# In the down half of a turn ScalarE rounds the weight pieces of a step before the squared activations of that step

## Chip, cores and metric

The kernel runs on one core of one Trainium2 chip. The metric is the device time of one launch in microseconds, and the time of a kernel is the median of its runs.

## The reference

One layer of a decoder trunk with two parallel branches, for 1024 positions of width 1024, in float32. The branches, their gates and the output projection come first. The change lies in the last part, the feed-forward layer with a squared ReLU:

```python
z = rmsnorm(h, norm_mlp[l])
h = h + jnp.square(jax.nn.relu(z @ w_up[l])) @ w_down[l]     # 1024 -> 4096 -> 1024
return rmsnorm(h, norm_final)
```

## The kernel before

**Numbers in two parts.** TensorE multiplies rounded numbers (fp32r). To keep the precision, every operand x is split into a high part, hi = x rounded, and a low part, lo = x - hi. One product is then three matmuls: hi·hi, hi·lo and lo·hi (lines 799 to 801). The high part of an operand is a Copy activation of ScalarE. The low part is a subtraction on VectorE or on GpSimd, which must wait for the high part.

**Turns and steps.** The first 512 of the 4096 hidden features are done by two plain blocks. The other 3584 are done in 7 turns of 512 features. A turn forms its 2x2 block products by seven products instead of eight (`PRODUCTS`, a Strassen-like scheme), so that sums and differences of weight blocks ("pieces") and of activation quarters are needed. A turn has 28 steps (`PIECES = 28`), and TensorE does 12 matmuls in each. The steps 0 to 13 are the up half (z times pieces of `w_up`, into the PSUM tile `aux`). The steps 14 to 27 are the down half: product m (0 to 6) has two steps, k = 0 and 1. In step 14 + q, with q = 2m + k, TensorE takes the squared activations number q from the slot q % 3 of `h_ring` as stationary operand, and piece 14 + q as moving operand, and adds to `acc` (m even) or `aux` (m odd).

**The five engines.** All of them run the same steps s = 0 to 27 with their instructions in an order written out by hand, and semaphores hold them together. Each engine executes in order, so an instruction that waits holds up everything behind it.

- SyncE loads piece p into its slot of a ring of 7 raw buffers (`p_a`, `p_b`, `p_c`) when TensorE has finished with piece p - 7 (`released`).
- GpSimd (`pieces`) forms the sums of pieces (lines 767, 774, 778; in `sum_at` it is fixed at which step), and the low parts of the pieces 0 to 2 and 18 to 27 (line 756; `lo_at`). Within a step the low parts come first and then the sums. From step 14 on its order is: sum 18 (step 14), sums 19 and 20 (15), low part 18 and sum 21 (16), low parts 19 and 20 and sum 22 (17), low part 21 and sum 23 (18), low parts 22, 23 and so on, low part 27 and sum 29 (24), low part 28 (25), low part 29 and sums 30 and 31 (26). Pieces from 28 on are the pieces 0, 1, ... of the next turn.
- ScalarE (`win_block` in its program) copies and squares quarters in the up half. It rounds the pieces (`cast_pieces(s)`, line 1761: the piece p with `cast_at(p) == s`) and the squared activations (`hidden_hi(q)`, line 1805, in step s = q + 12 for q from 3 on). The cast of piece 18 belongs to step 15, those of 19 and 20 to step 16, then one piece in each step to step 25, and 30 and 31 in step 27.
- VectorE forms the low parts of the pieces 3 to 17 (line 2595), those of the activations (`hidden_lo(q)`, line 2602, in step q + 12), the sums and differences of activation quarters (`hidden_s3`, `hidden_s1`, `hidden_s2`, `hidden_s4`, lines 2609, 2614, 2619, 2625), and it adds finished products from PSUM to the residual `h_res` (`add_pair`, line 2634, 1024 columns in one instruction). Its order around the change is: low parts 1 and 2 of the activations (step 14); `hidden_s3(1)`, `hidden_s1(1)`, `hidden_lo(3)`, `add_pair(0, 0)` (15); `add_pair(0, 1)`, `hidden_s2(1)`, `hidden_lo(4)` (16); `hidden_lo(5)`, `add_pair(1, 0)` (17); and at the end of the turn `hidden_s4(0)`, `hidden_lo(12)` (24) and `hidden_s4(1)`, `hidden_lo(13)` (25).
- TensorE starts step 14 + q when piece 14 + q has its low part (`piece_ready`) and `hidden_lo(q)` is done (`h_ready`).

`hidden_hi(3)` reads the difference that `hidden_s3(1)` writes, and `hidden_hi(5)` what `hidden_s2(1)` writes; `hidden_hi(12)` and `hidden_hi(13)` read what the two `hidden_s4` write. The others only need that TensorE is done with the slot of `h_ring`:

```python
if q >= HRING:
    released(act, UP_PIECES + q - HRING, g)      # TensorE has done step 14 + q - 3
sums = {1: (1, 4), 2: (3, 6), 4: (2, 5), 6: (7, 8)}.get(m)
```

Of the kernel before, what the change touches and what calls it, by code (L numbers as in the profile page):

```python
# [75 lines left out]
def kind(p):  # L76

    r = p % PIECES
    return r % N_PROD if r < UP_PIECES else (r - UP_PIECES) // 2


def chain_of(p):

    r = p % PIECES
    return r // N_PROD if r < UP_PIECES else r % 2
# [6 lines left out]
def cast_at(p):  # L92
    return p - (3 if kind(p) == 2 else 4)
# [6 lines left out]
def summed(p):  # L100
    return SUMS * (p // PIECES) + sum(kind(x) in (1, 2, 3, 4) for x in range(p % PIECES + 1))
# [65 lines left out]
def build(nc, t):  # L167
    with ExitStack() as ctx:
# [298 lines left out]
        def ring(p):  # L467

            s = p % RING
            slot = t_a[:, s] if s < 4 else t_b[:, s - 4] if s < 6 else t_c[:]  # L470
            return slot[:, 0, :], slot[:, 1, :]

        def piece_raw(p):
            s = p % RING
            return (p_a[:, s] if s < 4 else p_b[:, s - 4] if s < 6 else p_c[:])[:, 1, :]

        def released(eng, p, g):

            r, turn = p % PIECES, p // PIECES
            if r < UP_PIECES:  # L480
                eng.wait_ge(prod, g * UP_PIECES + (UP_PIECES * turn + r + 1))
            elif r % 2 == 0:
                eng.wait_ge(half_way, g * N_PROD + (N_PROD * turn + kind(r) + 1))
            else:
                eng.wait_ge(out_ready, g * PIECES + (PIECES * turn + OUT_WIN + 4 * (kind(r) + 1)))

        def quarter(q, k):
            return hid_raw[:, q, k, :]
# [837 lines left out]
        def _(act):  # L1326
# [424 lines left out]
            def cast_pieces(s, g, more=True):  # L1751

                for p in range(s, s + 5):
                    if p >= 0 and (p < PIECES or more) and cast_at(p) == s:
                        if kind(p) in (1, 2, 3, 4):
                            act.wait_ge(t_summed, g * SUMS + summed(p))
                        else:
                            act.wait_ge(ring_in[p % RING], g * 64 + 16 * (p // RING + 1))
                        hi, lo = ring(p)
                        src = t_raw[:, chain_of(p), :] if kind(p) in (1, 2) else piece_raw(p)  # L1760
                        nc.scalar.activation(hi, src, ACT.Copy).then_inc(t_cast, 1)  # L1761
# [11 lines left out]
            def win_block(g, more):  # L1773

                def copy(s, i):
                    q, bank = ((Q11, (0, 3)[s]), (Q22, 1), (Q21, (0, 3)[s]))[i]
                    act.wait_ge(prod, g * 14 + (7 * s + i + 1))
                    nc.scalar.activation(quarter(q, s), aux[:, bank, :], ACT.Copy).then_inc(copied, 1)

                def square(s, i):  # L1780
                    q = (Q21, Q22, Q11, Q12)[i]
                    n = 4 * s + i + 1
                    if i < 3:
                        act.wait_ge(taken, g * 6 + (3 * s + i + 1))
                        nc.scalar.activation(quarter(q, s), quarter(q, s), ACT.Relu).then_inc(relued, 1)
                    else:
                        act.wait_ge(prod, g * 14 + (7 * s + 7))
                        nc.scalar.activation(quarter(q, s), aux[:, (0, 3)[s], :], ACT.Relu).then_inc(u_taken, 1)
                        act.sem_inc(relued, 1)
                        act.wait_ge(u_taken, g * 2 + (s + 1))  # L1790
                    act.wait_ge(relued, g * 8 + n)
                    nc.scalar.activation(quarter(q, s), quarter(q, s), ACT.Square).then_inc(squared, 1)

                def hidden_hi(q):
                    m, k = q // 2, q % 2
                    hi, lo = h_ring[:, q % HRING, 0, :], h_ring[:, q % HRING, 1, :]
                    if q >= HRING:
                        released(act, UP_PIECES + q - HRING, g)
                    sums = {1: (1, 4), 2: (3, 6), 4: (2, 5), 6: (7, 8)}.get(m)
                    if sums is not None:  # L1800
                        act.wait_ge(h_summed, g * 8 + sums[k])
                    else:
                        act.wait_ge(squared, g * 8 + (SQUARED + 4 * k + {0: 3, 3: 2, 5: 4}[m]))
                    src = h_sum[:, q % HRING, 1, :] if m in (1, 6) else quarter({0: Q11, 2: Q11, 3: Q22, 4: Q21, 5: Q12}[m], k)
                    nc.scalar.activation(hi, src, ACT.Copy).then_inc(h_cast, 1)  # L1805

                for s in range(PIECES):
                    if s == 8:
                        hidden_hi(0)
                    if 15 <= s <= 25:  # L1810
                        hidden_hi(s - 12)
                    for b in range(2):
                        if 1 <= s - 7 * b <= 3:
                            copy(b, s - 7 * b - 1)
                        if 4 <= s - 7 * b <= 7:
                            square(b, s - 7 * b - 4)
                    if s == 13:
                        hidden_hi(1)
                        hidden_hi(2)
                    cast_pieces(s, g, more)  # L1820

            with act.Fori(0, N_WIN - 1) as g:
                win_block(g, True)
            win_block(N_WIN - 1, False)

            last_adds = OUT_WIN + 14 * (N_WIN - 1)
# [973 lines left out]
```

## Time and profile before

| what | value |
|---|---|
| time, median of 3 runs | 1497.07 us (1497.02 to 1497.55) |
| profiled execution: time, span | 1496.87 us, 1494.8 us |
| granted TensorE clock, mean | 0.995 |
| TensorE busy | 1465.8 us, 98% |
| VectorE, ScalarE, GpSimd busy | 66%, 35%, 35% |
| the seven turns | from about 933 us to about 1477 us of the span, 77.7 us each |

The span is that of the profiled execution, from its first to its last instruction; its own time is 2.1 us longer. Busy shares are of the whole span. In rows of the timeline the first number is the start in us from the beginning of the span and the second the time that the instruction took. That time contains whatever held the instruction after it had been issued, which matters below.

### The profile page before, as it was taken

What the parts mean: (1) busy time and instruction counts of PE and PEld (TensorE: products, weight loads), DVE (VectorE), ACT (ScalarE), POOL (GpSimd) and SP (SyncE); (2) the same over time, 40 slices, a digit from 0 to 9 for tenths busy, and PEclk for the clock granted to TensorE, in tenths of its full rate; (3) what the DMA queues carried; (4) which work ended last, traced back from release to release, by engine and by line L of the source; (5) the groups of instructions that cost most, each with busy time, mean ns of one, the idle gap of its engine ahead of it and who ended that gap; (6) DMA issues with size and microseconds to landing.
All of it is one profiled execution on the core that took longest, in us unless ns stands there. A gap on an engine that the chain in (4) does not pass through costs nothing.

```text
span 1494.8 us, 20639 instructions
## 1 busy us (share of the span) xinstructions
PE 1465.8 (98%) x7019; PEld 1210.5 (81%) x7019; DVE 981.0 (66%) x1911; ACT 517.9 (35%) x1003; POOL 519.2 (35%) x349
## 2 busy tenths in 40 slices
PE   9999999999999999999999999999999999999995
PEld 8887888888888888888888888878787878787874
DVE  6898564543467527675624788595958586767678
ACT  7422312400122212241101322545444444444455
POOL 4000001245332332004333003273737373646556
PEclk9999999999999999999999999999999999999998
DMA  7225543282111101003542001333333333333333
GB/s 221 99 90 143 144 109 124 72 279 88 57 43 43 43 29 57 29 29 131 179 176 71 1 29 50 120 99 116 103 112 106 104 108 107 108 107 110 107 111 135
DMA packets 150933, 149.02 MB, mean 100 GB/s; under 512 B 19104, under 2 KB 109904, under 8 KB 150864
## 3 DMA queue, kind: packets, MB, share of 16 engines
q1 hardware_dynamic: 118048, 107.00, 23.2%
q10 hardware_dynamic: 32816, 41.12, 8.5%
q8 instruction: 42, 0.69, 0.2%
q14 instruction: 27, 0.22, 0.0%
HBM read 126.58 MB, written 21.50 MB: 99 GB/s over the span
## 4 chain that ended last, share of the span: by engine, by line
PE 84%; DVE 9%; issue 3%; ACT 2%; POOL 1%; ACTq 1%; DMA 0%; DVEq 0%; POOLq 0%
PE acc L799 19%; PE acc L801 19%; PE acc L800 19%; PE aux L800 7%; PE aux L801 7%; PE aux L799 7%; DVE h_ring L2602 1%; DVE h_res L2634 1%; PE aux L1081 1%; PE aux L1074 1%; PE aux L1084 1%; DVE h_sum L2609 1%; PE aux L964 1%; PE aux L958 0%; PE aux L1069 0%
## 5 line engine op out<-in xcount | busy, mean ns | idle before, releaser
L799 PE MATMUL acc<-z_hi,w_hi 128*128 128x512 f32 x448 | 177.2, 396 | 0.6 <-DVE z_lo L1874 0.6
L801 PE MATMUL acc<-z_hi,w_lo 128*128 128x512 f32 x448 | 174.6, 390 | 0.0
L800 PE MATMUL acc<-z_lo,w_hi 128*128 128x512 f32 x448 | 174.5, 390 | 0.0
L799 PE MATMUL acc<-w_hi,z_hi 128*128 128x512 f32 x384 | 164.4, 428 | 0.0
L801 PE MATMUL acc<-w_hi,z_lo 128*128 128x512 f32 x384 | 150.5, 392 | 0.0
L800 PE MATMUL acc<-w_lo,z_hi 128*128 128x512 f32 x384 | 149.6, 390 | 0.0
L663 POOL CAST w_hi<-stage 128x1024 fp32r<-128x1024 f32 x22 | 27.7, 1259 | 344.2 <-PE acc L801 290.0
L650 POOL TENSOR_SCALAR stage<-stage,nm 128x512 f32<-128x512 f32 x48 | 78.3, 1643 | 168.8 <-PE acc L801 86.0
L767 POOL TENSOR_TENSOR t_raw<-t_raw,p_a 128x512 f32<-128x512 f32 x28 | 39.5, 1409 | 262.3 <-DMA p_a<-in_w_up 157.1
L799 PEld LDWEIGHTS acc<-z_hi,w_hi 128*128 128x128 f32 x448 | 84.1, 188 | 19.8 <-issue 1.5
L801 PEld LDWEIGHTS acc<-z_hi,w_lo 128*128 128x128 f32 x448 | 84.1, 188 | 17.9
L800 PEld LDWEIGHTS acc<-z_lo,w_hi 128*128 128x128 f32 x448 | 84.1, 188 | 16.8
L2589 DVE TENSOR_TENSOR hid_raw<-hid_raw,aux 128x512 f32<-128x512 f32 x42 | 28.9, 688 | 91.5 <-PE aux L801 91.5
L801 PEld LDWEIGHTS acc<-w_hi,z_lo 128*128 128x128 f32 x384 | 72.0, 188 | 16.2
L2602 DVE TENSOR_TENSOR h_ring<-hid_raw,h_ring 128x512 fp32r<-128x512 f32 x70 | 82.2, 1195 | 2.2 <-ACT h_ring L1805 2.2
L800 PEld LDWEIGHTS acc<-w_lo,z_hi 128*128 128x128 f32 x384 | 72.4, 189 | 13.5
L799 PEld LDWEIGHTS acc<-w_hi,z_hi 128*128 128x128 f32 x384 | 72.2, 188 | 13.3
L2634 DVE TENSOR_TENSOR h_res<-h_res,acc 128x1024 f32<-128x1024 f32 x54 | 64.3, 1215 | 2.1 <-PE acc L801 1.7
L1805 ACT ACTIVATE h_ring<-hid_raw 128x512 fp32r<-128x512 f32 x70 | 43.7, 624 | 42.2 <-PE aux L801 19.0
L1761 ACT ACTIVATE t_a<-p_a 128x512 fp32r<-128x512 f32 x70 | 43.5, 622 | 36.8 <-POOL p_a L778 36.8
L665 POOL TENSOR_TENSOR w_lo<-stage,w_hi 128x1024 fp32r<-128x1024 f32 x22 | 55.0, 2500 | 1.8
L1459 ACT ACTIVATE gate_t<-acc 128x512 f32<-128x512 f32 x32 | 19.0, 593 | 105.4 <-PE acc L801 94.6
(417 smaller groups left out, 3879.7 us busy)
## 6 DMA issues: line engine op xcount, KB each, us to landing
stage<-in_w_in SPq DMA_DIRECT2D x28, 512.0 KB, 4.4
p_a<-in_w_up SPq DMA_DIRECT2D x56, 256.0 KB, 2.8
p_a<-in_w_down SPq DMA_DIRECT2D x56, 256.0 KB, 2.6
gate_dram<-gate_t ACTq DMA_DIRECT2D x32, 256.0 KB, 2.1
p_b<-in_w_up SPq DMA_DIRECT2D x28, 256.0 KB, 2.7
p_b<-in_w_down SPq DMA_DIRECT2D x28, 256.0 KB, 2.7
x_in<-in_x SPq DMA_DIRECT2D x8, 512.0 KB, 6.1
stage<-in_w_in SPq DMA_DIRECT2D x32, 128.0 KB, 2.3
```

Of the source, the lines that this page charges most:

```text
L650: ins = nc.gpsimd.tensor_scalar(w[:, i, :], w[:, i, :], nm[:, k0 + i:k0 + i + 1], None, ALU.mult)
L663: nc.gpsimd.tensor_copy(dst_hi, stage[:, s, :]).then_inc(hi_pool, 1)
L665: nc.gpsimd.tensor_tensor(dst_lo, stage[:, s, :], dst_hi.bitcast(F32), ALU.subtract)\
L767: ins = nc.gpsimd.tensor_tensor(tmp_raw, tmp_raw, raw_lo, ALU.subtract)
L799: nc.tensor.matmul(out, s_hi, m_hi_, start=first, stop=False, skip_group_check=partial)
L800: nc.tensor.matmul(out, s_hi, m_lo_, start=False, stop=False, skip_group_check=partial)
L801: return nc.tensor.matmul(out, s_lo, m_hi_, start=False, stop=last, skip_group_check=partial)
L1761: nc.scalar.activation(hi, src, ACT.Copy).then_inc(t_cast, 1)
L1805: nc.scalar.activation(hi, src, ACT.Copy).then_inc(h_cast, 1)
L2589: V.tensor_tensor(quarter(q, s), quarter(q, s), aux[:, bank, :], ALU.add).then_inc(taken, 1)
L2602: V.tensor_tensor(lo, src, hi.bitcast(F32), ALU.subtract).then_inc(h_ready, 1)
L2634: V.tensor_tensor(rows, rows, (acc, aux)[m % 2][:, 2 * b:2 * b + 2, :], ALU.add).then_inc(out_free, 1)
```

## The change

In the steps 15 to 27 ScalarE executes `cast_pieces(s)` at the top of the step, ahead of `hidden_hi(s - 12)`. Before, it came last in the step. The steps 0 to 14 stay as they were. No instruction is added or removed, no semaphore count changes, and the other engines' programs are the same.

```diff
                 for s in range(PIECES):
                     if s == 8:
                         hidden_hi(0)
+                    if s >= 15:
+                        cast_pieces(s, g, more)
                     if 15 <= s <= 25:
                         hidden_hi(s - 12)
                     for b in range(2):
...
                     if s == 13:
                         hidden_hi(1)
                         hidden_hi(2)
-                    cast_pieces(s, g, more)
+                    if s < 15:
+                        cast_pieces(s, g, more)
```

## Rows read from the trace of the kernel before

**Rows 1.** The page: busy time of each engine over the span.

```profile
PE 1465.8 (98%) x7019; PEld 1210.5 (81%) x7019; DVE 981.0 (66%) x1911; ACT 517.9 (35%) x1003; POOL 519.2 (35%) x349
```

**Rows 2.** The waits from 900 to 1490 us: who waited for what.

```profile
PE acc L799 <- DVE h_ring L2602: 5.7, 5, 1.1
...
PE acc L799 <- POOL t_b L756: 2.1, 2, 1.1
```

**Rows 3.** The timeline of TensorE, second turn, around step 18.

```profile
1057.42 0.39 PE L799 MATMUL aux<-t_a,h_ring 128*128 128x512 f32 x1
...
1059.91 0.39 PE L801 MATMUL aux<-t_a,h_ring 128*128 128x512 f32 x1
1061.45 0.49 PE L799 MATMUL acc<-t_b,h_ring 128*128 128x512 f32 x1 [1.14 <-DVE h_ring L2602]
...
1064.31 0.39 PE L799 MATMUL acc<-t_b,h_ring 128*128 128x512 f32 x1
```

**Rows 4.** The timeline of the other engines, second turn, steps 14 to 17.

```profile
1048.88 1.30 POOL L774 TENSOR_TENSOR t_raw<-t_raw,p_b 128x512 f32<-128x512 f32 x1 [0.63 <-DVE t_a L2595]
...
1051.05 0.64 ACT L1792 ACTIVATE hid_raw<-hid_raw 128x512 f32<-128x512 f32 x1
...
1051.26 1.68 POOL L774 TENSOR_TENSOR t_raw<-t_raw,p_b 128x512 f32<-128x512 f32 x1 [1.09 <-DVE t_a L2595]
1051.70 1.79 DVE L2602 TENSOR_TENSOR h_ring<-h_sum,h_ring 128x512 fp32r<-128x512 f32 x1
1052.23 3.00 SPq L611 DMA_DIRECT2D p_a<-in_w_down  x2
1052.91 1.73 POOL L778 TENSOR_TENSOR p_c<-p_c,t_raw 128x512 f32<-128x512 f32 x1
1053.42 1.77 DVE L2609 TENSOR_TENSOR h_sum<-hid_raw 128x512 f32<-128x512 f32 x1
1055.22 0.69 DVE L2614 TENSOR_TENSOR hid_raw<-hid_raw 128x512 f32<-128x512 f32 x1
1055.29 0.63 ACT L1805 ACTIVATE h_ring<-h_sum 128x512 fp32r<-128x512 f32 x1 [3.60 <-DVE h_sum L2609]
1055.83 0.62 ACT L1761 ACTIVATE t_b<-t_raw 128x512 fp32r<-128x512 f32 x1
1055.95 0.69 DVE L2602 TENSOR_TENSOR h_ring<-h_sum,h_ring 128x512 fp32r<-128x512 f32 x1
...
1056.52 1.30 POOL L756 TENSOR_TENSOR t_b<-t_raw,t_b 128x512 fp32r<-128x512 f32 x1 [1.88 <-ACT t_b L1761]
1056.57 2.35 DVE L2634 TENSOR_TENSOR h_res<-h_res,acc 128x1024 f32<-128x1024 f32 x2
...
1058.83 0.79 DVE L2619 TENSOR_TENSOR hid_raw<-hid_raw 128x512 f32<-128x512 f32 x1
1059.03 1.74 POOL L756 TENSOR_TENSOR t_b<-t_raw,t_b 128x512 fp32r<-128x512 f32 x1
1059.54 1.77 DVE L2602 TENSOR_TENSOR h_ring<-hid_raw,h_ring 128x512 fp32r<-128x512 f32 x1
```

**Rows 5.** The page: DMA issues of down pieces, KB each, median us to landing.

```profile
p_a<-in_w_down SPq DMA_DIRECT2D x56, 256.0 KB, 2.6
```

**Rows 6.** The timeline, second turn, steps 24 to 27.

```profile
1079.22 1.29 POOL L767 TENSOR_TENSOR t_raw<-t_raw,p_a 128x512 f32<-128x512 f32 x1 [1.23 <-DMA p_a<-in_w_up]
1079.45 1.60 DVE L2625 TENSOR_TENSOR h_sum<-hid_raw 128x512 f32<-128x512 f32 x1
...
1082.38 1.29 POOL L756 TENSOR_TENSOR t_a<-p_a,t_a 128x512 fp32r<-128x512 f32 x1 [1.87 <-ACT t_a L1761]
1082.43 1.79 DVE L2625 TENSOR_TENSOR h_sum<-hid_raw 128x512 f32<-128x512 f32 x1
...
1084.98 0.69 DVE L2602 TENSOR_TENSOR h_ring<-h_sum,h_ring 128x512 fp32r<-128x512 f32 x1 [0.76 <-ACT h_ring L1805]
...
1086.07 0.39 PE L799 MATMUL acc<-t_c,h_ring 128*128 128x512 f32 x1
```

## The prediction, made before the changed kernel was built

> **What bounds the kernel now.** I read the page first, then the waits of TensorE in the seven turns, then the timeline around its one regular wait. TensorE is busy for 98% of the span [rows 1], so only its waits can be won or lost. From 900 to 1490 us it has seven waits of about 1.1 us, one in each turn, five put down to VectorE's low part of the activations and two to GpSimd's low part of a piece [rows 2]. The timeline of the second turn shows the place. Step 17 begins at 57.42 (I leave out the 1000 us of every time from here on), its last matmul starts at 59.91, and step 18 could begin 0.23 us later, at 60.14. It begins at 61.45 [rows 3]. The wait costs 1.31 us, and the first matmuls after it run slower: step 19 begins at 64.31, 2.86 us later, where a step takes 12 x 0.227 = 2.72 us (0.227 is the eleventh part of 57.42 to 59.91). So a wait costs 0.14 us on top.
>
> What comes last before 61.45 is `hidden_lo(4)`. VectorE has worked without a pause since the low part 2 at 51.70 [rows 4], so step 18 is set by how long VectorE's instructions take. Their times say more: the same 512 columns take 0.69 us (55.22, 55.95) or 1.7 to 1.8 us (51.70, 53.42, 59.54). A long one overlaps a GpSimd instruction and ends 0.55 us after it. GpSimd ends at 52.94, VectorE at 53.49. GpSimd ends at 54.64, VectorE at 55.19. GpSimd ends at 60.77, VectorE at 61.31. The reverse holds too: GpSimd's instruction takes 1.30 us alone (56.52), but if VectorE is at work when it comes, it ends 1.15 us after VectorE's (53.49 to 54.64; 59.62 to 60.77). So the two engines take turns: when both have an instruction waiting, the one that has just finished comes second. Only `add_pair`, which reads one operand from PSUM, doesn't take part: it runs 2.35 us for two beside GpSimd's 1.30 us [rows 4].
>
> The Trainium skill, page "SBUF — State Buffer", section "Who interferes with whom", says that a VectorE instruction with two inputs in SBUF and a GpSimd instruction that reads SBUF block each other for the whole instruction. The trace agrees in the order. If each blocked instruction then needed its full time alone (0.69 and 1.30 us), each handover would cost 0.14 us more than the rows have, and my sum below, with 8 handovers, would be 1.1 us larger in a turn, 7.8 us in all; I use the rows.
>
> **What the change moves.** Twelve casts of a turn (pieces 18 to 29) go ahead of the `hidden_hi` of their step; nothing is added. ScalarE itself has room (35% busy [rows 1]). What counts is who waited for the moved casts.
>
> *The cast of piece 18.* Its source, sum 18, is done at 50.18 (48.88 + 1.30). ScalarE ends its last square at 51.69 and then sits idle 3.60 us for `hidden_s3(1)`, because `hidden_hi(3)` stands first; the cast follows at 55.83, and GpSimd, idle since 54.64, starts low part 18 at 56.52 with "1.88 <-ACT t_b L1761" [rows 4]. After the change the cast runs at about 51.7, and GpSimd goes on at 54.64 without a gap. That gap is what VectorE used for `hidden_s1(1)` and `hidden_lo(3)` at 0.69 us each. It is closed. I go through it with the two rules above:
>
> - `hidden_s3(1)` has waited since 53.42 and goes first: ends 55.19, as before. GpSimd's low part 18: 55.19 + 1.15 = 56.34.
> - `hidden_s1(1)`: 56.34 + 0.55 = 56.89. Sum 21: + 1.15 = 58.04.
> - `hidden_lo(3)` (its high part is still ready at 55.92): + 0.55 = 58.59. Low part 19: + 1.15 = 59.74.
> - Two `add_pair`, free of the other engine: 58.59 + 2.35 - 0.1 (adjacent starts overlap by so much) = about 60.85. GpSimd's low part 20 runs beside them: 59.74 + 1.26 = 61.00.
> - `hidden_s2(1)`: 61.00 + 0.54 = 61.54. Sum 22: + 1.15 = 62.69.
> - `hidden_lo(4)`: + 0.55 = 63.24, where it was 61.31.
>
> The casts of 19 and 20 now follow `hidden_hi(3)` (55.83, 56.35) and are in time; `hidden_hi(4)` moves by two casts to about 56.9, far ahead of its use. The DMA doesn't hold GpSimd: piece 22 is issued in the pair that starts at 52.23 and lasts 3.00 us [rows 4], and lands 2.6 us after its issue [rows 5], before 58; it is wanted at 61.
>
> TensorE: step 17 needs `hidden_lo(3)` and so begins at 58.59 + 0.14 = 58.73 instead of 57.42, a new wait of 1.3 us. Step 18 could then begin at 58.73 + 2.86 = 61.59, but begins at 63.24 + 0.14 = 63.38. Before it was 61.45: the turn loses 1.93 us. In all seven turns the wait is the same size [rows 2], so 7 x 1.93 = 13.5 us.
>
> *The casts of 21 to 27.* GpSimd gets them earlier against the sums, but it is already fully engaged there. Continuing the same way, `hidden_lo(5)` ends at 64.94 (step 19 at 66.2), `hidden_lo(6)` at 67.95 (step 20 at 68.96). About 1 us of cover stays in each; I cost them at nothing. If an additional GpSimd instruction fell ahead of each, it would just eat this 1 us.
>
> *The casts of 28 and 29*, in the old time of the turn. Before, they come after `hidden_hi(12)` and `hidden_hi(13)`, which wait for the two `hidden_s4`; GpSimd's low part 28 starts at 82.38 after 1.87 us of waiting, `hidden_lo(13)` ends at 85.67, and step 27 begins at 86.07 [rows 6]: 0.26 us of cover beyond the 0.14 from low part to matmul. After the change low part 28 follows sum 29 (79.22 + 1.29 = 80.51) and `hidden_s4(0)` (81.06): 82.21. `hidden_lo(12)` 82.76; low part 29 83.91; `hidden_s4(1)` 84.46; sum 30 85.61; `hidden_lo(13)` 86.16; step 27 at 86.30, so 0.23 us late plus 0.14 us of slow start, 0.37 us. The last turn has no pieces of a next one: 6 x 0.37 = 2.2 us. Between 0 and 0.5 us a turn are open here, as four handovers at 0.05 us of error decide.
>
> *Piece 30 on* comes earlier to the up half of the next turn, where nobody waited for it to TensorE's cost: nothing.
>
> Sum: 13.5 + 2.2 = 15.7 us. The profiled execution would go from 1496.87 us (span 1494.8) to 1512.6. The median of the runs is 0.2 us above that execution, so the forecast is **1512.8 us**, 1.0% slower. About 0.2% (3 us) is what a measurement of this kernel can tell from no change.
>
> **Rivals.**
>
> *GpSimd's head start helps* (other side). GpSimd's block comes 1.9 us earlier, so low parts 19 and 20 could be out of the way when `hidden_s2(1)` and `hidden_lo(4)` come. If `hidden_s1(1)` and `hidden_lo(3)` were not held by low part 18 and sum 21, `hidden_lo(4)` would end at about 60.1 and the wait of 1.31 + 0.14 us would go: 7 x 1.45 = 10 us, 1487 us. It decides where the two run at 0.69 us with GpSimd at work. For it: step 18 is in two turns put down to GpSimd [rows 2]. Against it: every row of 0.69 us here is one without GpSimd beside it, or one that began before it. Chance 0.06.
>
> *The moved casts change nothing.* GpSimd would be held to 56.5 by something else (a DMA, the ring), or VectorE's order would win all the same: 1497. Against it: the wait row names the cast alone, and sum 21 ran directly behind low part 18. Chance 0.08.
>
> *One hold only.* VectorE loses the first exchange but gets two instructions through later; `hidden_lo(3)` is late by 1.2 to 1.5 us but `hidden_lo(4)` only by 0.9: 7 x 0.9 = 6, 1503 us. Chance 0.09.
>
> *More holds.* Each further GpSimd instruction ahead of `hidden_lo(4)`, `hidden_lo(6)` or `hidden_lo(13)` costs 1.15 to 1.3 us less what cover is left, some 8 us over the turns: 1521 us. Chance 0.07.
>
> **How the numbers follow.** The forecast has the chance 0.70, with its own range from 1508 (two handovers and the end of the turn cheaper) to 1517. The whole range is 1502 to 1520: it takes in the case of one hold, and leaves out the first two rivals and most of the last, some 0.18. Faster 0.06, same 0.08, slower 0.86.
>
> **What would show it.** The cast of piece 18 directly behind the last square, 1.88 us of waiting gone from low part 18. Line 2614's instruction at 1.7 us in step 15. TensorE waits twice in a turn, by about 1.2 us at step 17 and 1.6 us at step 18, and a turn of 80.0 us for 77.7. The forecast is wrong if `hidden_s1(1)` stays at 0.69 us, or if GpSimd doesn't follow on at 54.64.

## The result, and the profile after

The changed kernel takes 1512.28 us (median of 5 runs, 1511.9 to 1514.53), the kernel before 1497.25 us beside it (1497.02 to 1497.55): a ratio of 1.0103, 95% interval 1.0089 to 1.0117, 15.0 us slower. The forecast was 1512.8 us, in a range of 1502 to 1520. In the profiled executions the span grew from 1494.8 to 1510.3 us.

The page of the changed kernel, busy time by engine, beside [rows 1]:

```profile
span 1510.3 us, 20639 instructions
...
PE 1469.3 (97%) x7019; PEld 1209.3 (80%) x7019; DVE 979.2 (65%) x1911; ACT 519.4 (34%) x1003; POOL 530.6 (35%) x349
```

The number of instructions is the same and so is nearly every engine's busy time. What grew is TensorE's waiting. Its waits from 900 to 1505 us, beside [rows 2] (the new lines of the diff move the line numbers of VectorE by 3):

```profile
PE acc L799 <- DVE h_ring L2605: 8.4, 5, 1.7
PE aux L799 <- DVE h_ring L2605: 7.5, 7, 1.1
...
PE acc L799 <- issue: 3.4, 3, 1.6
```

There are now two kinds: one into `aux` (step 17, seven times 1.1 us) and one into `acc` (step 18, up to 1.7 us). Two of the three waits put down to "issue" are step 18 too, 1.6 us each in the first and the last turn, so that each of the seven turns has both. TensorE's timeline in the second turn, beside [rows 3]; the last row is the start of step 27:

```profile
1059.71 0.39 PE L801 MATMUL aux<-t_a,h_ring 128*128 128x512 f32 x1
1061.18 0.50 PE L799 MATMUL aux<-t_a,h_ring 128*128 128x512 f32 x1 [1.08 <-DVE h_ring L2605]
...
1065.89 0.49 PE L799 MATMUL acc<-t_b,h_ring 128*128 128x512 f32 x1 [1.65 <-DVE h_ring L2605]
...
1090.63 0.50 PE L799 MATMUL acc<-t_c,h_ring 128*128 128x512 f32 x1
```

And the other three engines there, beside [rows 4]:

```profile
1053.59 0.63 ACT L1792 ACTIVATE hid_raw<-hid_raw 128x512 f32<-128x512 f32 x1
...
1054.13 0.62 ACT L1761 ACTIVATE t_b<-t_raw 128x512 fp32r<-128x512 f32 x1
...
1055.95 1.78 DVE L2612 TENSOR_TENSOR h_sum<-hid_raw 128x512 f32<-128x512 f32 x1
1057.15 1.74 POOL L756 TENSOR_TENSOR t_b<-t_raw,t_b 128x512 fp32r<-128x512 f32 x1
1057.77 1.67 DVE L2617 TENSOR_TENSOR hid_raw<-hid_raw 128x512 f32<-128x512 f32 x1
...
1058.85 1.73 POOL L778 TENSOR_TENSOR p_a<-p_a,t_raw 128x512 f32<-128x512 f32 x1
...
1059.36 1.77 DVE L2605 TENSOR_TENSOR h_ring<-h_sum,h_ring 128x512 fp32r<-128x512 f32 x1
...
1060.55 1.73 POOL L756 TENSOR_TENSOR t_b<-t_raw,t_b 128x512 fp32r<-128x512 f32 x1
...
1061.06 2.34 DVE L2637 TENSOR_TENSOR h_res<-h_res,acc 128x1024 f32<-128x1024 f32 x2
1062.25 1.29 POOL L756 TENSOR_TENSOR t_c<-p_c,t_c 128x512 fp32r<-128x512 f32 x1
1063.32 0.77 DVE L2622 TENSOR_TENSOR hid_raw<-hid_raw 128x512 f32<-128x512 f32 x1
1063.50 1.71 POOL L778 TENSOR_TENSOR p_a<-p_a,t_raw 128x512 f32<-128x512 f32 x1
1064.01 1.75 DVE L2605 TENSOR_TENSOR h_ring<-hid_raw,h_ring 128x512 fp32r<-128x512 f32 x1
```

The rows close like a zip. Wherever both engines have an instruction waiting, the GpSimd row (POOL) ends 1.15 us after the VectorE row (DVE) ahead of it, and the VectorE row 0.55 us after the GpSimd row ahead of it. The last row is `hidden_lo(4)`, which step 18 waits for: it ends at 1065.76, and step 18 begins at 1065.89. Low part 18 (1057.15) no longer waits for ScalarE; `hidden_s1(1)` (1057.77) takes 1.67 us where it took 0.69.

**Where the 15 us went.** From one step 18 to that of five turns later the changed kernel needs 1465.27 - 1065.89 = 399.38 us, 79.88 a turn; before it was 77.66 (61.45 in the second turn to 1449.76 in the seventh). Of the 2.22 us, 1.91 lie at the steps 17 and 18. The remaining 0.31 are put down to step 27, the only other place of a turn where a matmul begins later than before: 0.34 to 0.47 us after the one ahead of it instead of 0.23. With 7 x 1.91 + 6 x 0.31 = 15.2 us the turns hold all of it.

### The profile page after: what moved, and what is told of

It reads as the page before. It is cut to its first block, busy times and chain, and to the rows that moved or that the text cites. A ratio compares the mean times of both kernels' runs of the same rounds, so it can differ in the third digit from the quotient of the medians.

```text
span 1510.3 us, 20639 instructions
## 1 busy us (share of the span) xinstructions
PE 1469.3 (97%) x7019; PEld 1209.3 (80%) x7019; DVE 979.2 (65%) x1911; ACT 519.4 (34%) x1003; POOL 530.6 (35%) x349
## 4 chain that ended last, share of the span: by engine, by line
PE 83%; DVE 10%; issue 3%; ACT 2%; POOL 1%; ACTq 1%; DMA 0%; DVEq 0%; POOLq 0%
PE acc L799 19%; PE acc L801 18%; PE acc L800 18%; PE aux L799 7%; PE aux L801 7%; PE aux L800 7%; DVE h_ring L2605 2%; PE aux L1081 1%; DVE h_sum L2612 1%; PE aux L1074 1%; PE aux L1084 1%; DVE h_res L2637 1%; POOL h_res L792 1%; PE aux L964 1%; PE aux L958 0%
## 5 line engine op out<-in xcount | busy, mean ns | idle before, releaser
L799 PEld LDWEIGHTS acc<-w_hi,z_hi 128*128 128x128 f32 x384 | 72.2, 188 | 13.3
L2605 DVE TENSOR_TENSOR h_ring<-hid_raw,h_ring 128x512 fp32r<-128x512 f32 x70 | 70.7, 1029 | 10.9 <-ACT h_ring L1805 10.9
L756 POOL TENSOR_TENSOR t_a<-p_a,t_a 128x512 fp32r<-128x512 f32 x35 | 57.8, 1668 | 0.0
L778 POOL TENSOR_TENSOR p_a<-p_a,t_raw 128x512 f32<-128x512 f32 x35 | 57.3, 1638 | 1.2
```

The lines of the kernel that those rows point to most:

```text
L756: nc.gpsimd.tensor_tensor(lo, src, hi.bitcast(F32), ALU.subtract).then_inc(t_ready, 1)
L778: ins = nc.gpsimd.tensor_tensor(raw_lo, raw_lo, tmp_raw, ALU.subtract)
L799: nc.tensor.matmul(out, s_hi, m_hi_, start=first, stop=False, skip_group_check=partial)
L2605: V.tensor_tensor(lo, src, hi.bitcast(F32), ALU.subtract).then_inc(h_ready, 1)
```

## Experiments

One note on the numbers. In some executions the part ahead of the turns is some 3 us longer, in kernels that don't differ there: the first matmul of the turns begins at 936.3 to 937.1 us in four of the profiled ones, and at 933.4 to 934.9 in the others. So beside the time, each experiment has the length of its last part in the profiled execution, from the first matmul of the turns to the end of the span: 561.34 us before (1494.8 - 933.46), 576.56 after, 15.2 us more. This is what I compare. One execution of each kernel stands behind it, and its spread was not measured. Against the differences of the medians it is off by 1.1 us at most, and by 1.7 us in the last row, where the five runs lie between 1508.8 and 1513.6 us.

| kernel | time, us | before beside it | ratio, 95% interval | last part, us | against before |
|---|---|---|---|---|---|
| new order in step 15 only | 1511.3 | 1497.62 | 1.0091, 1.0075 to 1.0106 | 574.7 | +13.4 |
| in 16 to 27 | 1502.12 | 1497.62 | 1.0035, 1.0021 to 1.0048 | 565.8 | +4.5 |
| in 24 and 25 | 1499.44 | 1497.62 | 1.0014, 1.0005 to 1.0023 | 562.5 | +1.2 |
| in 18 | 1500.67 | 1497.68 | 1.002, 1.0011 to 1.0029 | 564.7 | +3.4 |
| in 16, 17, 19 to 27 | 1506.01 | 1497.68 | 1.0052, 1.0039 to 1.0066 | 570.1 | +8.8 |
| before, one reading GpSimd instruction more | 1510.38 | 1497.9 | 1.0084, 1.007 to 1.0098 | 574.7 | +13.3 |
| before, one filling GpSimd instruction more | 1497.5 | 1497.9 | 0.9996, 0.9987 to 1.0005 | 561.3 | 0.0 |
| changed, low part 18 held | 1503.84 | 1497.62 | 1.0047, 1.0034 to 1.0061 | 567.7 | +6.4 |
| the same, old order in 18 | 1507.64 | 1497.68 | 1.0063, 1.005 to 1.0077 | 572.4 | +11.0 |
| before, low part 19 held | 1493.14 | 1497.9 | 0.9965, 0.9951 to 0.9979 | 556.9 | -4.4 |
| changed, low parts 18 and 19 held | 1511.76 | 1497.9 | 1.0086, 1.0072 to 1.01 | 576.9 | +15.5 |

### Which step of the change costs

A piece's *cast* is its rounding on ScalarE. The first three kernels apply the new order to some of the steps:

```diff
-                    if s >= 15:
+                    if s == 15:            # or: s >= 16; or: s in (24, 25)
                         cast_pieces(s, g, more)
...
-                    if s < 15:
+                    if s != 15:            # or: s < 16; or: s not in (24, 25)
                         cast_pieces(s, g, more)
```

> Only step 15 has the new order: the cast of piece 18 goes ahead of hidden_hi(3); all other steps are as in the kernel before. Theory (GpSimd's low part 18 starts two microseconds earlier, and VectorE's hidden_s1(1), hidden_lo(3), hidden_s2(1) and hidden_lo(4) then alternate with GpSimd): nearly all the loss of steps 17 and 18 is here, 7 x 1.9 = 13.3 us, 1510.5 us; two waits of TensorE in a turn, none at step 27. Rival (the delayed hidden_hi are what VectorE waits for): hidden_hi(3) isn't delayed by a cast that is over 3 us earlier, so 1497 us.

> The new order in the steps 16 to 27, the old one in step 15. Theory: GpSimd keeps its gap before low part 18, so step 18 begins as before; only the end of the turn costs, 6 x 0.31 = 1.9 us, 1499.1 us. One place is open: sum 22 still ends at the old time, so the cast of piece 22 and then hidden_hi(6) come only after it, some 4 us later than before, 0.05 us before low part 21 ends; if hidden_lo(6) misses that moment it loses a handover of 1.25 us, step 20 is 0.5 us late, and the time is 1502.5 us. Rival (the delayed hidden_hi hold VectorE): nearly the whole loss stays, 1510 to 1512 us.

> The new order in the steps 24 and 25 only (the casts of pieces 28 and 29). Theory: low part 28 follows sum 29 without a gap, four more handovers before hidden_lo(13), step 27 begins 0.2 us late and 0.1 us slower, in six turns: 1.9 us, 1499.1 us. Rival (the end of the turn costs nothing, and the small late start of step 27 in the changed kernel is a remainder of what happened in steps 17 and 18): 1497.2 us.

Step 15 alone gives +13.4 us, as 7 x 1.91 does, with the waits of the changed kernel:

```profile
PE acc L799 <- DVE h_ring L2605: 8.3, 5, 1.7
PE aux L799 <- DVE h_ring L2605: 7.5, 7, 1.1
```

So one cast of the twelve, that of piece 18, by itself gives nearly nine tenths of the loss, and it is the one that could not have delayed anything on ScalarE, which was idle. The rival, that the delayed `hidden_hi` are what costs, is out for this part. The end of the turn costs +1.2 us by itself, 1.8 us by the medians, where 1.9 was expected; the interval leaves no change out.

The steps 16 to 27 give +4.5 us, not the 1.9 of the plain theory: the place that was left open decided the other way (1502.5 us was the figure for that, 1502.12 came). After the cast of piece 22 has waited for its sum, `hidden_hi(6)` follows:

```profile
1063.90 2.34 DVE L2637 TENSOR_TENSOR h_res<-h_res,aux 128x1024 f32<-128x1024 f32 x2
1065.10 1.30 POOL L756 TENSOR_TENSOR t_a<-p_a,t_a 128x512 fp32r<-128x512 f32 x1
1065.17 0.63 ACT L1761 ACTIVATE t_a<-p_a 128x512 fp32r<-128x512 f32 x1 [3.85 <-POOL p_a L778]
1065.71 0.61 ACT L1805 ACTIVATE h_ring<-hid_raw 128x512 fp32r<-128x512 f32 x1
1066.36 1.85 DVE L2605 TENSOR_TENSOR h_ring<-hid_raw,h_ring 128x512 fp32r<-128x512 f32 x1
1066.37 1.28 POOL L778 TENSOR_TENSOR p_a<-p_a,t_raw 128x512 f32<-128x512 f32 x1
```

`hidden_lo(6)` starts at 1066.36, low part 21 ends at 1066.40 and sum 23 starts at 1066.37. The sum goes first and takes its 1.28 us as if alone, and `hidden_lo(6)` ends 0.56 us after it, at 1068.21. Step 20 begins late at 1068.33. By the handover price `hidden_lo(6)` would have ended at 1066.95 had it gone first, so the order is worth some 1.2 us here; that is an estimate, as in no run did it go first from such a start.

### The steps 18 and 19 by themselves

```diff
-                    if s >= 15:
+                    if s == 18:            # or: s >= 16 and s != 18
                         cast_pieces(s, g, more)
...
-                    if s < 15:
+                    if s != 18:            # or: s < 16 or s == 18
                         cast_pieces(s, g, more)
```

> The new order in step 18 only: the cast of piece 22, which waits for GpSimd's sum 22, goes ahead of hidden_hi(6). Theory: hidden_hi(6) ends 4.0 us later and hidden_lo(6) misses the end of low part 21, loses a handover of 1.25 us, and step 20 is 0.35 us late and slower by 0.1 us: 7 x 0.43 = 3.0 us, 1500.6 us. Rival (step 20 was late only because of the shifts that steps 16, 17 and 19 make together): 1497.6 us.

> The new order in the steps 16, 17 and 19 to 27, the old one in 15 and 18. Theory: only the end of the turn is left, 6 x 0.25 = 1.5 us, 1499.1 us, and no wait at step 20. Rival (the casts ahead of hidden_hi(7) to hidden_hi(11) cost too): 1502 us, as with step 18.

Step 18 alone costs what was worked out (3.0 us expected, +3.4). The second kernel is a miss: without the new order in step 18 the loss grows to +8.8 us instead of shrinking to 1.5. There the same happens one step later, and worse. With the old order in step 18 `hidden_lo(6)` is in time and goes ahead of sum 23, which therefore takes 1.74 us and not 1.28. The timeline of its second turn:

```profile
1067.13 1.74 POOL L778 TENSOR_TENSOR p_a<-p_a,t_raw 128x512 f32<-128x512 f32 x1
...
1068.90 0.63 ACT L1761 ACTIVATE t_a<-p_a 128x512 fp32r<-128x512 f32 x1 [2.33 <-POOL p_a L778]
...
1069.44 0.61 ACT L1805 ACTIVATE h_ring<-hid_raw 128x512 fp32r<-128x512 f32 x1
...
1070.09 1.83 DVE L2605 TENSOR_TENSOR h_ring<-hid_raw,h_ring 128x512 fp32r<-128x512 f32 x1 [2.38 <-ACT h_ring L1805]
```

The cast of piece 23 waits for its sum (1067.13), `hidden_hi(7)` waits behind the cast, and VectorE stands still for 2.38 us before `hidden_lo(7)`, which then takes 1.83 us beside GpSimd (1.03 with the new order in 16 to 27). Step 21 then begins 0.5 us late (0.73 us after the matmul before it, for 0.23) and step 22 is 0.2 us late too. So the rival, that a cast ahead of `hidden_hi` holds the activations up, is right for the steps 18 and 19, where a cast has to wait for GpSimd's sum. It doesn't show in the changed kernel, where VectorE itself comes to these instructions 1.9 us later: `hidden_hi(6)` is done there at 1066.39 and `hidden_hi(7)` at 1069.79, `hidden_lo(6)` starts only at 1069.64, behind `add_pair`, and `hidden_lo(7)` follows it without a gap.

### The loss without touching ScalarE

If GpSimd's earlier work is the cause, another GpSimd instruction in that gap must do the same to the kernel before. Behind sum 20:

```diff
                         ins.then_inc(t_summed, 1)
+                if t == 15:
+                    pool.wait_ge(t_summed, g * SUMS + summed(19))
+                    nc.gpsimd.tensor_tensor(tmp[:, 2, :], t_raw[:, 0, :], t_raw[:, 1, :],
+                                            ALU.subtract)
```

and, in the second kernel, `nc.gpsimd.memset(tmp[:, 2, :], 0.0)` in the same place without the wait.

> The kernel before, with ScalarE's old order, and one GpSimd instruction more in a turn, directly behind sum 20: a subtraction of two SBUF tiles of 128x512 into an unused one (about 1.3 us, in GpSimd's idle time of 1.88 us; nobody uses its result). Theory (VectorE and GpSimd alternate): it costs what the change costs at the steps 17 and 18, as hidden_s1(1) and hidden_lo(3) are held: 7 x 1.9 us = 13.3 us and no loss at step 27, 1510.5 us; up to 1513 us as GpSimd has 1.15 us more to do before low part 22. Rival (the loss comes from ScalarE's order): 1497 us, as the instruction fits into the idle time.

> The same place, but the extra GpSimd instruction fills the unused 128x512 tile with zeros: it writes SBUF and reads nothing. Theory in its narrow form (the two engines hold each other only where GpSimd reads SBUF): hidden_s1(1) and hidden_lo(3) stay at 0.69 us, 1497 us. Theory in its wide form (any GpSimd instruction that touches SBUF): hidden_s1(1) is held until the fill ends, a loss of one handover at least, 1503 to 1511 us.

The reading instruction costs 13.3 us, the filling one nothing. The zip in the kernel with the reading one (line 782 is the added instruction):

```profile
1056.77 1.74 POOL L782 TENSOR_TENSOR tmp<-t_raw 128x512 f32<-128x512 f32 x1
1057.40 1.67 DVE L2618 TENSOR_TENSOR hid_raw<-hid_raw 128x512 f32<-128x512 f32 x1
```

and the same place with the filling one:

```profile
1053.65 1.77 DVE L2611 TENSOR_TENSOR h_sum<-hid_raw 128x512 f32<-128x512 f32 x1
1054.81 0.53 POOL L781 MEMSET tmp<- 128x512 f32 x1
1055.46 0.69 DVE L2616 TENSOR_TENSOR hid_raw<-hid_raw 128x512 f32<-128x512 f32 x1
```

The fill runs beside `hidden_s3(1)` with 0.53 us, inside VectorE's 1.77, and neither it nor `hidden_s1(1)` behind it is stretched. This bears out the narrow form of the rule, that the two hold each other where GpSimd reads SBUF. The Trainium skill says so too ("SBUF — State Buffer", section "Who interferes with whom": a VectorE instruction with two SBUF inputs contends with a GpSimd instruction that reads SBUF, "not with one that only writes it"). The trace agrees as far as it reaches: the fill takes 0.52 to 0.53 us in all seven turns, and `hidden_s3(1)` ends 0.55 us after sum 20, as without it. A caution: the fill is short and had ended when `hidden_s1(1)` began, so the 0.69 us of that instruction and the 0.0 us over the kernel would not show it alone. A filling instruction as long as the reading one wasn't run.

### Holding GpSimd back

```diff
                     if lo_at(p) == t and p % PIECES not in V_PIECES:
+                        if p == 18:
+                            pool.wait_ge(h_ready, g * 14 + 4)      # hidden_lo(3) done
+                        if p == 19:
+                            pool.wait_ge(h_ready, g * 14 + 5)      # hidden_lo(4) done
```

The changed kernel with the first wait, with the first wait and the old order in step 18, and with both; and the kernel before with the second alone.

> The changed kernel with one wait more: GpSimd begins low part 18 only when hidden_lo(3) is done. ScalarE keeps the new order in every step. Theory: the gap in GpSimd's work is back, hidden_s1(1) and hidden_lo(3) take 0.69 us, step 17 has no wait, step 18 begins as before; what stays is the end of the turn: 1499.1 us. Rival (ScalarE's order is what costs): 1512 us stays, or more, as a wait is added.

> The changed kernel with GpSimd's low part 18 held behind hidden_lo(3), and with the old order in step 18. Theory: of the 6.4 us that the turns lost with that wait alone, the 3.0 us at step 20 go; the 0.28 us a turn stay by which the wait starts low part 18 later than the kernel before (1.9 us), and the end of the turn (1.5 us): 1501 us. Rival (the rest has another cause): 1504 us as without it.

> The kernel before, with one wait more: GpSimd begins low part 19 only when hidden_lo(4) is done. Theory: hidden_lo(4) isn't held by low part 19 any more and ends at about 60.2 instead of 61.3 (second turn, 1000 us left out); step 18 begins 1.1 us earlier, nearly without a wait; low part 19 then ends at 61.5, needed at 63.1. A gain of 7 x 1.1 = 7.7 us, 1489.5 us. Rival (GpSimd then falls behind, and its low parts 21 to 27 come too late): 1497 us or slower.

> The changed kernel with both waits (low part 18 behind hidden_lo(3), low part 19 behind hidden_lo(4)). Theory: as the kernel before with the one wait at low part 19, plus the end of the turn: 1489.5 + 1.9 = 1491.4 us. Rival (ScalarE's order costs by itself): 1500 us or more.

The first wait takes back 8.8 of the 15.2 us, but not all that was expected (1503.84 us for 1499.1): in its second turn `hidden_s1(1)` and `hidden_lo(3)` take 0.69 us again and step 17 doesn't wait. What is left (+6.4 us) is the late `hidden_hi(6)` at step 20, the end of the turn, and 0.28 us a turn at step 18, since low part 18 starts after `hidden_lo(3)` and not beside it. With the old order in step 18 on top, 1501 us was expected and 1507.64 came, for the reason of the miss above: `hidden_hi(7)` behind the cast of piece 23.

The second wait makes the kernel before a little faster: 1493.14 us, ratio 0.9965 (0.9951 to 0.9979), 4.8 us less. Its `hidden_s2(1)` and `hidden_lo(4)` on VectorE, and TensorE's step 18:

```profile
1061.40 0.80 DVE L2621 TENSOR_TENSOR hid_raw<-hid_raw 128x512 f32<-128x512 f32 x1
1062.12 0.68 DVE L2604 TENSOR_TENSOR h_ring<-hid_raw,h_ring 128x512 fp32r<-128x512 f32 x1
...
1062.92 0.49 PE L801 MATMUL acc<-t_b,h_ring 128*128 128x512 f32 x1
```

`hidden_lo(4)` takes 0.68 us instead of 1.77, and step 18 begins 0.46 us after the matmul before it instead of 1.54. That was worth 7.7 us by the theory. Of these, 4.4 arrive. A turn gains 0.8 us (76.88 us from the second turn's step 18 to the third's, for 77.66); most of what is missing to 1.1 is lost at step 27, which in most turns now begins 0.33 to 0.42 us after the matmul before it and not 0.23, with a second matmul as slow. And the last turn gives 1.5 us back: there TensorE takes the steps 26 and 27 in alternation, needs `hidden_lo(13)` sooner, and begins step 26 2.04 us after the matmul before it (0.57 before). In that turn `hidden_lo(8)` starts in the same hundredth as a low part of GpSimd (1455.95) and takes 1.86 us, for 0.78 in the kernel before, and VectorE keeps this loss to `hidden_lo(13)`.

Both waits in the changed kernel are a miss, 1511.76 us for 1491.4: the cast of piece 22 waits longer still (4.42 us in the second turn, for 3.85 with the first wait alone), `hidden_hi(6)` and `hidden_lo(6)` behind it, and step 20 begins 1.8 to 2.0 us late in every turn.

## Why the prediction was right

**The first exchange.** Every step of the sum can be laid beside the trace, with 2.53 us taken off for the shift that the second turn has already (`hidden_s3(1)` starts at 1055.95 for 1053.42). Predicted and measured ends: low part 18 56.34 and 56.36, `hidden_s1(1)` 56.89 and 56.91, sum 21 58.04 and 58.05, `hidden_lo(3)` 58.59 and 58.60, low part 19 59.74 and 59.75, the two `add_pair` 60.85 and 60.87, low part 20 61.00 and 61.01, `hidden_s2(1)` 61.54 and 61.56, sum 22 62.69 and 62.68, `hidden_lo(4)` 63.24 and 63.23. Step 17 was forecast for 58.73 and began at 58.65, step 18 for 63.38 and began at 63.36. The term, 1.93 us, measured 1.91. The handover prices of 0.55 and 1.15 us, taken from five places in the rows before, held.

**The end of the turn** was forecast at 0.37 us and measured 0.31 a turn, in the changed kernel as a whole, as what is left of the 2.22; by itself (steps 24 and 25) it came to 0.2. `hidden_lo(13)` ended at 86.16 by the sum. In the trace it ends at 1090.57, which less 2.53 and 1.91 is 86.13.

**The casts of 21 to 27 at nothing.** The figure is right for the changed kernel, but its reason was incomplete. I looked at them as things that GpSimd gets earlier. I didn't ask what stands behind a cast that waits for a sum. The experiments show that step 18 costs 3.4 us alone and that the steps 16, 17 and 19 to 27 cost 8.8, most of it at the steps 21 and 22. That it cost nothing in the changed kernel was then partly luck, as the sum had no term for it. The loss of step 15 covers these costs: 13.4 and 4.5 us add up to 17.9, where the whole change costs 15.2. They are not additive: the late `hidden_hi` cost nothing only where VectorE is late already.

**The rivals.** GpSimd's head start does not help: `hidden_s1(1)` is at 1.67 us. "Nothing changes" and "one hold only" (1503 us) are out by the interval and by the rows, and "more holds" (1521 us) by the time. That the late `hidden_hi` on ScalarE cost something was not among my rivals; it is real, and hidden here.

**What the Trainium skill states** ("SBUF — State Buffer", section "Who interferes with whom") gave who holds whom, and not the price: with full times alone at each handover the forecast would be 7.8 us more, 1520.6 us, an estimate. In the rows above the blocked instruction ends some 0.14 us sooner than that.

**Open.** Whether the steps 24 and 25 cost less alone (1.2 us by the last part, 1.8 by the medians) than in the changed kernel (1.9) wasn't settled, nor how the 4.5 us of the steps 16 to 27 divide between step 20 and the end of the turn beyond the waits read off TensorE's timeline.

## What to carry to other kernels

An idle gap on an engine with room can be what keeps another engine fast. Before an instruction is released earlier, look whether the work behind it shares something with the engine on the critical path: here VectorE's instructions were 0.69 us in GpSimd's gap and 1.7 us beside it, and a wait of GpSimd of 1.9 us in each of seven turns was worth 13 us. The cure is the reverse: make the engine with room wait while the critical one has its burst (4.8 us here), and count what its own backlog pushes back later. On an engine that runs in order, put an instruction that waits for a third engine behind those whose operands are ready.

## What the runs showed that I had not expected

- A near tie went to GpSimd. In the kernel with the new order in 16 to 27 `hidden_lo(6)` started at 1066.36 and sum 23 at 1066.37, both while low part 21 was just ending at 1066.40; the sum went first, and `hidden_lo(6)` took 1.85 us. With the first wait in the changed kernel the same pair starts at 1069.37 and 1069.38 and goes the same way. Where VectorE had been waiting for 0.2 us or more in the rows shown, it went first.
- TensorE's clock. In the changed kernel with both waits step 18 begins 0.5 to 0.75 us and step 20 2.0 to 2.2 us after the matmul before it. In the second, fourth and sixth turn the granted clock then fell to its lower level of 1.2 GHz for some 3.5 us, matmuls 0.43 us apart instead of 0.23:

```profile
1070.70:1074.20 3.50, 3.50 (x10) 2.69 (x9) 3.50 (x4) 1.39 (x3) 3.50 (x4) 0.51 0.00 0
```

  (The row gives the length, the busy time and count of PE, PEld, DVE, ACT and POOL, the granted clock, the DMA share and GB/s.) In the other four turns, with such waits too, it did not fall, nor behind the waits at the steps 17 and 18 of the changed kernel, where 1.5 and 2.0 us lie between the matmuls. What decides it, the runs don't show.
